# A fused decoder step with a top-4-of-32 expert layer: GpSimd's row gathers and row scatters issued in turn

## The reference, cut to what matters

```python
logits = h @ w_router + b_router               # (544, 32)
top_v, top_i = lax.top_k(logits, 4)
gates = softmax(top_v)
# for each expert e, on the rows h[t] of the tokens that chose it:
g = minimum(x @ w_gate[e] + b_gate[e], 7)
u = clip(x @ w_up[e] + b_up[e], -7, 7)
y = ((u + 1) * g * sigmoid(1.702 * g)) @ w_down[e] + b_down[e]
# out[t] += gate * y ; then x = x + g2 * out, and a final RMSNorm
```

## Time and profile before

| what | value |
|---|---|
| timed runs | 1334.65, 1336.98, 1338.87 us, median 1336.98 us |
| span of the profiled execution | 1348.8 us |
| TensorE busy | 1287.5 us, 95% of the span |
| VectorE, ScalarE, GpSimd busy | 517.3 us (38%), 90.2 us (7%), 242.2 us (18%) |
| mean granted TensorE clock | 0.984 |
| DMA | 487.60 MB, mean 362 GB/s |

### The profile page before, as it was taken

How to read it: one execution, slowest core, us unless ns; L and a number is a source line. 1 busy time by engine, 2 the same in 40 slices (tenths; PEclk the granted TensorE clock), 3 DMA queues, 4 the chain that set the end, 5 groups by cost and what they waited for, 6 DMA issues and landing times.

```text
span 1348.8 us, 32006 instructions
## 1 busy us (share of the span) xinstructions
PE 1287.5 (95%) x14057; PEld 744.1 (55%) x14057; DVE 517.3 (38%) x813; ACT 90.2 (7%) x165; POOL 242.2 (18%) x315
## 2 busy tenths in 40 slices
PE   4999999779999999999999999999999999999997
PEld 2787754514655655555554555544555555555674
DVE  1213213542333444444433333333334444444446
ACT  3200011200000000000000000000000000000002
POOL 4001300062111111111122221111111111111110
PEclk9999999789999999999999999999999999999999
DMA  9885960356999999999999999999999999999993
GB/s 327 256 327 212 346 246 32 149 224 248 411 410 423 405 413 407 409 410 405 421 407 411 411 416 410 407 408 409 425 417 406 400 421 407 416 401 424 418 411 154
DMA packets 64294, 487.60 MB, mean 362 GB/s; under 512 B 11911, under 2 KB 21607, under 8 KB 38917
## 3 DMA queue, kind: packets, MB, share of 16 engines
q1 hardware_dynamic: 47442, 455.92, 83.2%
q0 software_dynamic: 11264, 19.96, 4.1%
q10 hardware_dynamic: 5555, 11.25, 2.3%
HBM read 468.41 MB, written 25.97 MB: 367 GB/s over the span
## 4 chain that ended last, share of the span: by engine, by line
PE 93%; DVE 2%; issue 2%; DMA 2%; ACT 1%; SPq 0%; POOL 0%; DVEq 0%; POOLq 0%; ACTq 0%
PE acc L1877 52%; PE acc L1900 23%; PE acc L945 9%; PE acc L989 4%; PE acc L862 2%; DMA raw<-in_w_ada 1%; PE acc L1981 1%; PE acc L1000 1%; PE acc L880 1%; ACT h_t L488 1%; PE acc L1997 0%; DVE picked L1593 0%; PE acc L961 0%; DMA rows<-h_rows,row_first 0%; DVE raw_b L1586 0%
## 5 line engine op out<-in xcount | busy, mean ns | idle before, releaser
L1877 PE MATMUL acc<-raw_b,ht 128*32 128x512 f32 x3024 | 381.2, 599 | 16.4 <-issue 13.0
L1877 PE MATMUL acc<-raw,ht 128*32 128x512 f32 x2928 | 339.0, 592 | 0.0
L1877 PEld LDWEIGHTS acc<-raw_b,ht 128*32 128x32 f32 x3024 | 142.0, 111 | 235.1 <-issue 231.2
L1650 DVE TENSOR_TENSOR g_sb<-acc,bias_gu 128x768 f32<-128x768 f32 x32 | 30.6, 957 | 570.4 <-PE acc L1877 570.4
L1877 PEld LDWEIGHTS acc<-raw,ht 128*32 128x32 f32 x2928 | 151.6, 110 | 156.6 <-issue 149.8
L1391 POOL DMA_INDIRECT rows<-h_rows,row_next x90 | 91.3, 1014 | 742.1 <-DVE row_next L1542 722.7
L1900 PE MATMUL acc<-raw_b,at 128*32 128x256 f32 x2976 | 183.7, 379 | 0.0
L1900 PE MATMUL acc<-raw,at 128*32 128x256 f32 x2976 | 183.7, 379 | 0.0
L1900 PEld LDWEIGHTS acc<-raw_b,at 128*32 128x32 f32 x2976 | 135.7, 110 | 42.2 <-issue 9.8
L1900 PEld LDWEIGHTS acc<-raw,at 128*32 128x32 f32 x2976 | 133.5, 109 | 32.1
L945 PE MATMUL acc<-h_t,raw 128*128 128x288 f32 (+1 forms) x512 | 118.3, 393 | 1.1 <-DVE h_t L702 1.1
(11 more groups left out here) (249 smaller groups left out, 639.8 us busy)
## 6 DMA issues: line engine op xcount, KB each, us to landing
raw<-in_w_down SPq DMA_DIRECT2D x33, 2048.0 KB, 15.5
raw<-in_w_gate SPq DMA_DIRECT2D x31, 2048.0 KB
raw<-in_w_up SPq DMA_DIRECT2D x31, 2048.0 KB
raw_b<-in_w_gate SPq DMA_DIRECT2D x31, 2048.0 KB
raw_b<-in_w_up SPq DMA_DIRECT2D x31, 2048.0 KB
raw_b<-in_w_down SPq DMA_DIRECT2D x31, 2048.0 KB
raw<-in_w_ada SPq DMA_DIRECT2D x24, 1024.0 KB, 12.1
expert_rows<-zeros ACTq DMA_DIRECT2D x1, 8704.0 KB, 30.4
```

Of the source, the lines that this page charges most:

```text
L1650: dve.tensor_tensor(g_sb[:, :, :], gate_of(i, 0), plus(0), ALU.add).then_inc(g_read, 1)
L1877: mm = pe.matmul(gu_of(i)[b][q * TB:(q + 1) * TB, :].rearrange("p (m n) -> p m n", m=2), ht_of(i)[:, b, k, :], w[:, kk, :, q * CW:(q + 1) ...
```

## The change

In steps 2 to 30 GpSimd no longer issues three gathers and then three scatters, but gather, scatter, gather, scatter, gather, scatter, by block. The two waits that stood ahead of the three scatters now stand behind the first gather. Steps 0 and 1 (gather only) and step 31 (scatter only) stay as they are, as do the six transfers of a step themselves.

```diff
+                def gather_block(e, b):
+                    idx = row_first[e] if isinstance(e, int) and e < 2 else row_next
+                    pool.indirect_dma_start(rows[:, b, :], None, h2_quarter,
+                                            bass.IndirectOffsetOnAxis(ap=idx[:, b:b + 1], axis=0),
+                                            bounds_check=Q * NTOK - 1, oob_is_err=False).then_inc(row_gathered, 16)
+
+                def scatter_waits(e):
                     pool.wait_ge(y_scaled, e + 1)
                     pool.wait_ge(y_idx_ready, e + 1)
                     if not isinstance(e, int):
                         pool.nop(nofuse=True)
+
+                def scatter_block(b):
+                    pool.indirect_dma_start(y_quarter, bass.IndirectOffsetOnAxis(ap=y_idx[:, b:b + 1], axis=0),
+                                            y_sb[:, b, :], None, bounds_check=Q * ROWS - 1, oob_is_err=False)\
+                        .then_inc(y_stored, 16)
...
                 def step(i):
-                    if not (isinstance(i, int) and i == E - 1):
+                    early = isinstance(i, int) and i < 2
+                    last = isinstance(i, int) and i == E - 1
+                    if early:
                         gather(i + 1)
-                    if not (isinstance(i, int) and i < 2):
+                    elif last:
                         scatter(i - 2)
+                    else:
+                        gather_waits(i + 1)
+                        for b in range(SB):
+                            gather_block(i + 1, b)
+                            if b == 0:
+                                scatter_waits(i - 2)
+                            scatter_block(b)
```

More of the change, by code:

```diff
@@ L1380, in _, with gather_waits @@
                 pool.wait_ge(rows_filled, 1)
-                def gather(e):
+                def gather_waits(e):
                     pool.wait_ge(id_ready, e + 1)
@@ L1386, in gather @@
                         pool.wait_ge(ht_ready, e)
-                    idx = row_first[e] if isinstance(e, int) and e < 2 else row_next
                     if not isinstance(e, int):
                         pool.nop(nofuse=True)
[L1390 to L1395, removed]
+                def gather_block(e, b):
[4 more added lines that the diff above has]
+                def scatter_waits(e):
                     pool.wait_ge(y_scaled, e + 1)
@@ L1400, in scatter, with gather @@
                         pool.nop(nofuse=True)
-                    for b in range(SB):
-                        pool.indirect_dma_start(y_quarter, bass.IndirectOffsetOnAxis(ap=y_idx[:, b:b + 1], axis=0),
-                                                y_sb[:, b, :], None, bounds_check=Q * ROWS - 1, oob_is_err=False)\
-                            .then_inc(y_stored, 16)
+                def scatter_block(b):
+                    pool.indirect_dma_start(y_quarter, bass.IndirectOffsetOnAxis(ap=y_idx[:, b:b + 1], axis=0),
+                                            y_sb[:, b, :], None, bounds_check=Q * ROWS - 1, oob_is_err=False)\
+                        .then_inc(y_stored, 16)
+                def gather(e):
+                    gather_waits(e)
+                    for b in range(SB):
+                        gather_block(e, b)
+                def scatter(e):
+                    scatter_waits(e)
+                    for b in range(SB):
+                        scatter_block(b)
                 def step(i):
-                    if not (isinstance(i, int) and i == E - 1):
+                    early = isinstance(i, int) and i < 2
+                    last = isinstance(i, int) and i == E - 1
+                    if early:
                         gather(i + 1)
-                    if not (isinstance(i, int) and i < 2):
+                    elif last:
                         scatter(i - 2)
+                    else:
+                        gather_waits(i + 1)
+                        for b in range(SB):
+                            gather_block(i + 1, b)
+                            if b == 0:
+                                scatter_waits(i - 2)
+                            scatter_block(b)
                 gather(0)
```

## The result

| | median us | runs | ratio to before, 95% interval |
|---|---|---|---|
| before, beside it | 1337.38 | 1334.65 to 1338.87 (4) | |
| after | 1323.28 | 1322.22 to 1325.33 (4) | 0.9895 (0.9882 to 0.9909) |

A forecast was written before the change was run, and what follows sets the result against it. The prediction took TensorE, 93% of the chain and nearly balanced with full DMA engines, to bound the kernel. Every term was 0, so it forecast 1337 us, no change, with a range of 1331 to 1344 us.

The forecast's parts named there:

- What bounds the kernel: Expert loop: TensorE is 93% of the chain; a step takes 31.94 us, 0.98 beyond TensorE's own 30.96.
- The wait that moved: GpSimd's second DMA of a step, now a scatter waiting for y_scaled and y_idx_ready: both ready about 0.3 us before, cost 0.
- The sum of 0: All terms together: no change on a span of 1348.8 us, forecast 1337 us.
- my own signs of being wrong: turn_rows released by a gather's DMA, q0's share outside 3.5 to 5%, or mean step moving by more than 0.15 us.
- The gathers come later: Third gather issued at 711.4 instead of 708.8 us; 8 to 12 us remain before turn_rows reads it, cost 0.
- the scatters come earlier or as before: First scatter issued at 707.45 instead of 710.07 us, third as before; step 31's isn't moved, gain 0.
- The transfers' order on the DMA engines: Same bytes beside other weights: taken as 0, bounded by 18.7 us gained in 29 steps and 33 us lost.
- Faster: mixing helps: Pause in mid gate_up: thinner scatter traffic might shorten it, a quarter of 28.4 us, 7 us: 1330 us; chance 0.08.
- my own bound of 1318 us: Low end of the transfer order's unknown cost, left out of the range as needing the weights' lead to count for nothing.
- the scatter that runs in front of the weights: DMA engines at 711 to 714 us: weights land up to 0.3 us later each step, 8.7 us: 1346 us; chance 0.10.
- scatters holding gathers: GpSimd's queue: gathers wait for scatters' 7.0 us completion; all six in turn lose 7.3 us a step, about 1549 us; chance 0.02.
- the wait for y_scaled comes late: GpSimd's second DMA: two gathers pushed back together, even 12 us costing nothing, 1337 us; chance 0.02.

The follow-up runs named there:

- e1: Kernel before with only the scatter's two waits moved behind the first gather, the order of the six transfers unchanged: 1323.30 us, ratio 0.9781.
- e5: Kernel before with TensorE's loop over experts 2 to 31 written out, GpSimd unchanged: 1351.72 us, ratio 1.0003.
- e3b: Kernel before with each scatter of steps 2 to 30 replaced by a plain 64-byte transfer on the same queue: five runs, 1323.29 to 1353.23 us.
- e10: Kernel before plus a GpSimd clearing of 512 columns of a spare tile between the third gather and the first scatter: 1321.09 us, ratio 0.9858.
- e7: Kernel before with the scatter's two waits moved behind the second gather, order of transfers unchanged: 1339.42 us, ratio 0.9994.
- h3: e2 plus a GpSimd clearing of 512 columns behind its first scatter: 1322.58 us, ratio 0.9883.
- e2: Kernel before with the scatter's waits and three scatters put ahead of the gather's waits and three gathers: 1338.69 us, ratio 0.9902.
- h2: Kernel before plus a GpSimd clearing of 128 columns of a spare tile behind the first gather: 1331.17 us, ratio 0.994.

## Why the prediction was wrong, step by step

- **What bounds the kernel** was right: TensorE without a pause takes 30.96 us a step, a step paid 0.98 us more, 28.4 us in all, in mid gate_up. That is what went.
- **"The wait that moved ... Cost: 0"** is the step that failed. I compared when y_sb was ready (707.14) with when the second DMA could start (707.45) and took 0.31 us of margin for enough. But a start follows its semaphore late: 0.87 us in after. The trace of before shows as much, in the row below with the first gather of the earlier trace rows: row_next is done at 705.20 and the gather starts at 706.11, 0.91 us later. The gap of 0.30 us holds only between DMAs that GpSimd has already been let through to. With 0.9 us, the second DMA would have been put at 707.14 + 0.9 = 708.0, 0.6 us late, which is what was measured. (Timeline of before.)

```profile
705.01 0.19 DVE L1542 TENSOR_SCALAR row_next<-table,q_col 128x3 uint32 x1
```

I had written that a cost there "would be tenths of a us on GpSimd, and the next point hides that". The size was about right, and for the gathers' landing it is hidden; that a delay could be a gain I didn't consider. The sum of 0 took TensorE's pause of 0.98 us a step as given, though I had no releaser for it. In its place the runs show 0.6 us of delay on GpSimd and the whole pause gone: 28.4 us in the profiled executions, 14.1 us in the medians. Two of my own signs of being wrong came about: VectorE held the second DMA for more than 0.1 us, and the mean step moved by 0.98 us.
- **The gathers come later, the scatters come earlier or as before**: no loss from either, as predicted; turn_rows waits for no gather. What I weighed of the Trainium skill ("DMA: Bandwidth & Descriptors", on the anatomy of a GpSimd DMA) is about when one transfer counts as complete. That it would hold the gather behind a scatter was my reading and not the page's words, and the trace speaks against it: that gather starts 1.32 us later (732.34 against 731.02) and turn_rows isn't held.
- **The transfers' order on the DMA engines** at 0: right. e1 has the old order and the whole gain, and q0's share is 4.1% (4.0 before).
- **"Faster: mixing helps"** had the place (the pause starts when the sixth DMA is issued) and the amount at stake (28.4 us), of which I priced a quarter at a chance of 0.08. Its mechanism, thinner scatter traffic, is wrong by e1. What I held against it, that step 20 had "the same six DMAs and no pause", was a misreading: the same six, but not at the same times. A look at GpSimd's rows in the one step that differed would have turned this objection into the strongest evidence.
- **The three other rivals**: the scatter that runs in front of the weights asked for a growing pause and scatters holding gathers for a step of 39 us; neither came about. The last one, that the wait for y_scaled comes late, did come about in its condition (chance 0.02), by 0.6 us; its price, 1337 us, was wrong, since it looked at the gathers' margins alone.
- **Bounds**: the low end of the range left out my own bound of 1318 us, since it needed "the weights' lead to count for nothing". The pause was not about the weights' lead at all.

**What stays open.** Shown is that the pause depends on when GpSimd starts its last DMAs, in steps of 0.1 us, for two orders of transfers. Its size isn't set by that alone: in before, with the sixth DMA at 9.4 us each time, steps took 31.4, 31.7 or 32.2 us. Not shown is by what means. The trace gives "issue" alone: TensorE's instructions come late though its weights are there (by the trace's semaphore events the pair for the second half lands 4 to 7 us into the step, while TensorE reaches it at 9 us or later). The fetch of instructions over the DMA queues is out by e5 and before. Whether GpSimd's act of issuing or the packets that follow it disturb TensorE is open, since every delay moved both; e3b, where three small transfers in the scatters' place leave no pause, changed both too.

SP's rows show that more than TensorE's matmuls is held up. SP issues a step's first pair when TensorE reports the end of the step before, and the next pair when it reports the first half of gate_up. In step 13 of before the two lie 11.51 us apart. In step 13 of e10, which doesn't pause (timeline of SP):

```profile
690.92 0.33 SPq L1319 DMA_DIRECT2D raw<-in_w_down  x1
702.23 0.33 SPq L1319 DMA_DIRECT2D raw<-in_w_gate  x1
```

That is 11.31 us, and in e1, without a pause as well, 11.82 (696.88 and 708.70), but in after 10.31 (695.67 and 705.98). So TensorE's report reaches SP about a microsecond late in kernels with the pause and in some without it; TensorE itself stops only in the former. What a late report and a pause have in common isn't known.

Why before stands at 1337 to 1339 in some comparisons and at 1350 in others is open too; a pause of half the size would do it ((1338.61 - 1323.18) / 29 = 0.53 us a step), and e7, profiled at 1342.99 us, had 0.68 us.

## What to carry to other kernels

A wait for a semaphore isn't free because its semaphore comes in time for the end of the instruction ahead; take the delay from semaphore to start from a row where the engine did wait. When the chain shows a short pause marked "issue" that recurs at the same place of each step, look for the one step that lacks it and compare every engine's start times in the two, before the argument says that an engine with 0% of the chain can't matter. And a dummy instruction on the idle engine, a few tenths of a microsecond long, is a cheap test of such a coupling: if time moves although nothing else was moved, the order of the work is not needed to explain it.

## What the runs showed of the hardware that I had not expected

- TensorE paused for 0.5 to 1.0 us a step, or not at all, by whether GpSimd's last three indirect DMAs started 0.4 us later (e10, and h3 against e2); 0.1 us later took away half (h2).
- An indirect DMA of GpSimd starts about 0.9 us after the instruction that it waits for has ended (0.87 and 0.91 in the rows above), but 0.30 us after the DMA ahead of it when it has nothing to wait for; a clearing of 512 columns (0.54 us) in between delays the next by only 0.4 us, and three clearings, by 1.8 us whether the third has 64 or 512 columns.
- At steps of 30.96 us the core takes 424 GB/s with a DMA share of 1.01, and TensorE is busy throughout (31.00 of 31.00 us); no variant's median came below 1321 us.
